# Causal attention: the output products of two neighbouring key blocks issued in every second step

## The reference, cut to what matters

```python
def block(args):
    i, qi, ci = args
    qpos = i * Q_BLOCK + jnp.arange(Q_BLOCK)
    s = jnp.einsum('bhqd,bhkd->bhqk', qi, k, preferred_element_type=jnp.float32) * scale
    s = s + ci[..., :, None] - c[..., None, :]
    s = jnp.where(kpos[None, :] <= qpos[:, None], s, -jnp.inf)
    p = jax.nn.softmax(s, axis=-1)
    return jnp.einsum('bhqk,bhkd->bhqd', p.astype(v.dtype), v)
```

## Time and profile before

| | |
|---|---|
| median of 3 runs | 3397.64 us (3387.78 to 3401.16) |
| the profiled execution | 3401.32 us, span 3399.5 us |
| PE busy | 3210.6 us, 94% of the span |
| DVE, ACT, POOL busy | 38%, 28%, 7% |
| first causal stage, first matmul to last output of DVE | 256.85 to 390.75 us |
| second causal stage, end of its last products | 1220.34 us |

### The profile page before, as it was taken

The page is one execution under the profiler, slowest core; times in us unless marked ns, Lnnn a source line. Parts: engine busy times, 40 slices in busy tenths (PEclk is TensorE's granted clock), DMA queues, the critical chain, the costliest instruction groups (busy, mean ns, idle before and its releaser), DMA issues. The chain is left out here.

```text
span 3399.5 us, 39981 instructions
## 1 busy us (share of the span) xinstructions
PE 3210.6 (94%) x16110; PEld 2170.6 (64%) x16110; DVE 1286.3 (38%) x1773; ACT 958.2 (28%) x1570; POOL 236.9 (7%) x361
## 2 busy tenths in 40 slices
PE   7999999999999999999997899999997999999996
PEld 5886678888787667888786465444436556544442
DVE  4425554242532564333366552111116655111112
ACT  3325433132422633323242521000004542100001
POOL 1004200000100410000000200000000320000000
PEclk9999999999999999999997999999998999999999
DMA  5310123321441022323211235999992113799997
GB/s 158 119 55 26 66 85 98 99 87 62 130 137 38 1 88 86 99 88 98 77 49 23 76 112 218 426 427 427 427 422 86 64 54 118 304 426 427 427 427 308
DMA packets 234295, 590.22 MB, mean 174 GB/s; under 512 B 42962, under 2 KB 146328, under 8 KB 184996
## 3 DMA queue, kind: packets, MB, share of 16 engines
q1 hardware_dynamic: 234148, 588.15, 45.8%
HBM read 581.81 MB, written 2.10 MB: 172 GB/s over the span
## 5 line engine op out<-in xcount | busy, mean ns | idle before, releaser
L2574 PE MATMUL ps<-w_ring,xe 128*64 128x512 f32 x1024 | 233.7, 602 | 18.8 <-DMA w_ring<-in_w 13.8
L422 DVE TENSOR_TENSOR mlp_w_lo<-w_ring,mlp_w_hi 128x2048 fp32r<-128x2048 f32 x62 | 142.1, 2292 | 212.7 <-ACT mlp_w_hi L382 212.7
L357 PE MATMUL ps<-h_hi,in_w_hi 128*128 128x512 f32 (+1 forms) x528 | 207.0, 392 | 2.7 <-DVE h_lo L430 2.7
L357 PE MATMUL ps<-h_lo,in_w_hi 128*128 128x512 f32 (+1 forms) x528 | 205.7, 390 | 0.0
L357 PE MATMUL ps<-h_hi,in_w_lo 128*128 128x512 f32 (+1 forms) x528 | 205.6, 389 | 0.0
L357 PE MATMUL ps<-h_hi,mlp_w_hi 128*128 128x512 f32 x512 | 202.6, 396 | 2.1 <-DVE h_lo L430 2.1
L357 PE MATMUL ps<-h_hi,mlp_w_lo 128*128 128x512 f32 x512 | 202.5, 396 | 0.0
L357 PE MATMUL ps<-h_lo,mlp_w_hi 128*128 128x512 f32 x512 | 202.5, 395 | 0.0
L357 PE MATMUL ps<-mlp_w_hi,u_lo 128*128 128x512 f32 x512 | 202.3, 395 | 0.0
L357 PE MATMUL ps<-mlp_w_lo,u_hi 128*128 128x512 f32 x512 | 202.2, 395 | 0.0
L357 PE MATMUL ps<-mlp_w_hi,u_hi 128*128 128x512 f32 x512 | 202.2, 395 | 0.0
(11 more groups left out here) (551 smaller groups left out, 6153.2 us busy)
## 6 DMA issues: line engine op xcount, KB each, us to landing
ex_front<-in_w SPq DMA_DIRECT2D x192, 1024.0 KB, 17.5
w_ring<-in_w SPq DMA_DIRECT2D x128, 1024.0 KB, 20.7
ex_back<-in_w SPq DMA_DIRECT2D x64, 1024.0 KB, 19.8
w_ring<-in_w_in SPq DMA_DIRECT2D x32, 1024.0 KB, 5.4
w_ring<-in_w_up SPq DMA_DIRECT2D x32, 1024.0 KB, 5.4
w_ring<-in_w_down SPq DMA_DIRECT2D x32, 1024.0 KB, 5.0
w_ring<-in_cmp_w SPq DMA_DIRECT2D x16, 512.0 KB, 5.0
w_ring<-in_w_out SPq DMA_DIRECT2D x8, 1024.0 KB, 6.0
```

Source lines behind the costliest of these rows:

```text
L357: mm = pe.matmul(ps[0:o.rows, bank[k], 0:o.cols], lhsT, rhs, start=(o.first and j == 0), stop=(o.final and j == len(o.mm) - 1))
L422: dve.tensor_tensor(w.lo[:, home(n), 0:used], ring.slots[:, n % RING, 0:used], w.hi[:, home(n), 0:used].bitcast(F32), ALU.subtract).then_i ...
L2574: mm = pe.matmul(ps[rows, bank + half, :], lhsT, slot(2 * m + a)[:, kk, 512 * half:512 * half + 512], start=(k == 0), stop=(k == DC - 1))
```

## The change

In the causal stages the products of two neighbouring key blocks, kb = 0 and 1, then kb = 2 and 3, are issued together in the step where the second of them stood; in the other steps no product is issued. Each odd product keeps its step, each even one moves one step later. The full kind is left as it was.

```diff
--- before.py
+++ after.py
@@ -680,7 +680,11 @@
                         cmp_flip()
                     u = step - LAG - 1 - (TT - 1)
                     if 0 <= u < nu:
-                        mix(u // TT, u % TT)
+                        if kind == "full":
+                            mix(u // TT, u % TT)
+                        elif u % 2:
+                            mix(u // TT, u % TT - 1)
+                            mix(u // TT, u % TT)
                     if 0 <= step - LAG < nu:
                         flip(step - LAG)
```

## The result

The changed kernel takes 3413.83 us (median of 10 runs, 3405.16 to 3419.24) where the kernel before, beside it, takes 3397.16 us (10 runs, 3387.78 to 3403.59). The ratio is 1.0047, with a 95% interval of 1.0035 to 1.0058: 16.7 us slower by the medians, and clear of no change. The profiled execution took 3415.35 us, its span is 14.1 us longer than before.

A forecast was written before the change was run, and what follows sets the result against it. PE was taken as the bound in the causal stages; 20 cycles of +0.5 us (+10.0) and two tails (+0.6) made +10.6 on the median 3397.6, giving 3408 us, range 3391 to 3420.

The forecast's parts named there:

- The bound: Causal stages: PE is busy 19.67 of 20 us, so PE time saved is program time saved, barring new waits.
- The boundaries: PE, causal stages: each pair of products saves one change of array shape, 0.15 us, twice a cycle; 6.0 us over 40.
- the first rival: Causal stages: only the saved shape changes count, no new waits on PE; 3391 us, chance 0.13.
- Scores to flip as dear as scores to product: PE, twice a causal cycle: scores followed by a flip cost the same as by a product; bounds -4 to +2 us.
- Which copy decides: Causal cycle: flip 3 waits 0.65 us for ACT's copy 2, flip 2 waits 0.15 for copy 1.
- Product 2 follows and is through at 5.90 + 0.44 + 0.11: Causal cycle: product 2 starts at 5.90 us and is through at 6.45; only then can ACT make copy 2.
- Copy 0 (DVE, 0.42) waits for product 0, at 0.94 + 0.86 + 0.11 = 1.91: Causal cycle: DVE's copy of unit 0 into the transposed probabilities, 0.42 us long, waits for product 0 until 1.91 us.
- Copies that do not hold PE up: Causal stages: copy 2 ends before PE finishes product 3, so only boundaries count; 3391 us, chance 0.13.
- Queues that amplify: Causal stages: copy 0 delays maximum, exponentials and copy 1, 0.5 us more a cycle, 10 in all; 3418 us, chance 0.11.
- The clock: PE, causal stages: clock falls to 1.2 GHz for unit 2's flip and scores each cycle, 28 us more; 3436, chance 0.06.
- Rival B: Causal stages, posed after the result: two products in a row cost time on PE itself; no chance given.
- Exponentials behind the blocked copy 2, at nothing: ACT, causal stages: the next unit's exponentials queue behind copy 2 but are held up little; costed at nothing.

The follow-up runs named there:

- the first experiment: The changed product order with two sets of transposed probabilities in the causal stages, against the kernel before: 3393.27 us against 3399.11, ratio 0.9989.
- its control: The kernel before, old product order, given only two sets of transposed probabilities in the causal stages: 3399.07 us against 3399.31, ratio 1.0006.
- the turned pair: The changed kernel with product 3 issued ahead of product 2, copy 2 waiting for both: 3420.37 us in one run.

## Why the prediction was right, and what it mis-sized

- **The bound.** "So a microsecond saved on PE is a microsecond, if no new wait takes it": both halves hold. With two sets the saving arrives where nothing else holds PE up, with one set a wait takes it.
- **The boundaries.** 0.15 us each was right (1.65 for 1.80, and 0.80 for 0.96 where no copy disturbs the pair), and so was 0.30 a cycle, by the first experiment and its control (9.05 against 9.34), but only in cycles without an output copy or a compressed product. Times 40 it was too much: with two sets the two stages saved 4.2 us and not the 6.3 of the first rival, as the fox cycles gave little or nothing. In the change none of it is left: the first is used up by the wait of flip 1 for copy 0 (1.77 against 1.80), the second lies under the wait of flip 3.
- **Scores to flip as dear as scores to product.** Right, 0.24 us for either at full speed. It moved nothing, as both flips in question wait for a copy in the change.
- **Which copy decides.** Copy 2, ahead of flip 3, in each cycle, and copy 1 ahead of flip 2 in second place: right, shown by the runs with one pair each.
- **The term that was mis-sized**, while the mechanism was right, is "Product 2 follows and is through at 5.90 + 0.44 + 0.11", and with it the same 0.11 in "Copy 0 (DVE, 0.42) waits for product 0, at 0.94 + 0.86 + 0.11 = 1.91". The trace shows 0.33 in place of 0.11 in both: 353.80 - 352.61 = 1.19 for 0.86 of streaming, 358.51 - 357.75 = 0.76 for 0.43, and the turned pair gave it a third time. (The copies do not read the products; they overwrite what the products read, and wait for their end.) I took the 0.11 from a flip followed by scores, where it is counted from the start of the next block; but the start of the next block already holds 0.15 us of handing over. For a pair I took this 0.15 off the product, as PE no longer spends it, and took it off the time at which the product's end is seen as well, which still needs it. 0.07 more stays unexplained; it is not in every product, as the 0.26 at the end of a stage shows. So flip 3 came 1.67 us after product 2 began, not 1.46.
- **What followed from it.** With 0 at the start of flip 0: flip 1 at 2.68 (2.59 worked out), flip 2 at 4.29 (4.10), product 2 at 6.05 (5.90), copy 2 at 6.81 (6.45), flip 3 at 7.72 (7.36). Of these 0.36 us, 0.21 is product 2's result, and 0.15 the late copy 0, which holds flip 1 back and, through the maximum and the exponentials, copy 1. A cycle lost 0.85 us and not 0.50, a tail 0.56 and not 0.3; by the table 20 and 2 of them make 18.2 in place of 10.6. PE's wait ahead of flip 3 was 0.80 us, and 0.65 was forecast.
- **The rivals.** Copies that do not hold PE up: out. Queues that amplify: a part of it is real, the chain through copy 0 that was named there, at 0.15 us and not 0.5 a cycle. The clock: out, 1.00 throughout the steady part. Rival B, which came after the result, is out by four runs.
- **Exponentials behind the blocked copy 2, at nothing**: right. They start at 359.21 in the changed kernel, in the shadow of flip 3, and the scores that need them do not wait.
- **The total.** 3408 was forecast, 3413.8 is measured, in the range and slower, and the difference to the kernel before is 16.7 us instead of 10.6. It is just inside the 0.5% that was called the same, but the sentence that half a per cent "is about what a measurement of this kernel can tell from no change" did not hold: ten runs a side gave an interval of 0.35 to 0.58%. And "0.1 us in 20 cycles, spans 3402 to 3414" does not come out: 0.1 in 20 cycles is 2 us, which with the -4 to +2 of handing over gives 3402 to 3412. The 0.22 by which the product's end was mis-sized, twice a cycle, lies outside that allowance. So the total owes something to width: the stated range had been drawn for the rivals.

## What to carry to other kernels

Before work is grouped to save a switch, ask of each piece that moves later who waits for it: here the buffer of one set made product 2, once it was late, the thing that the next copy and flip waited for, and the switches saved (0.30 us a cycle) were a quarter of the waits gained (1.15). A buffer more made the same order a gain. Ask also what each piece that moves had covered: in the fox cycles and in gqa the flip left without a product ahead of it waited. And when the time saved at a boundary is taken off PE's own time, leave it in the time at which another engine sees the end of the work.

## What was not expected of the hardware

- A copy that waited for a product started 0.33 us later than the product's streaming time after its start, for 512 and for 256 columns alike (1.19 and 0.76 us), with another product behind it or with a block that waits itself. The output at the end of a stage was read after 0.26 us. No run has a copy waiting for a product with a flip running directly behind it.
- A change of the array's shape between two blocks cost PE 0.15 us: products 2 and 3 took 0.96 us apart and 0.80 together, and the compressed product of 32 rows took 1.00 us ahead of one of 128 rows in the same bank, where two of one shape need 0.86. In mla, eight transposes between scores of 96 rows took 0.88 us; in the other stages, with a change on either side, they take 0.99 to 1.02.
- The same four products took 4.06 us in one execution and 2.37 in another (the rows above), as the granted clock over them was 0.58 and 1.00. That is a tenth of this change's effect, and is one reason why cycle lengths in the trace told orders apart that the medians could not.
